# Post-norm residual of a two-layer transformer block: weights at evacuation, squares from the banks, one operation per token tile, two stores

## What is computed

```python
def _rms(x, g):
    xf = x.astype(jnp.float32)
    y = xf * lax.rsqrt(jnp.mean(xf * xf, axis=-1, keepdims=True) + EPS)
    return (y * g.astype(jnp.float32)).astype(x.dtype)

for l in range(DEPTH_2):
    mod = (silu_c @ w_ada[l] + b_ada[l])[:, None, :]
    ...
    y = _merge(o_lat[0], o_lat[1], o_lat[2], lam, lam_init, g_diff_sub[l]) @ w_out[l]
    x = x + gt_a * _rms(y, g_attn_post[l])
    ...
    hf = _rms(x, g_ffn_pre[l]) * (1.0 + sc_f) + sh_f
    x = x + gt_f * _rms(_swiglu(hf, w_ffn_gate[l], w_ffn_up[l], w_ffn_down[l]), g_ffn_post[l])
```

## Time and profile before

| | us |
|---|---|
| median of three runs (2558.07 to 2560.07) | 2558.24 |
| the profiled execution: time | 2554.62 |
| the profiled execution: span | 2552.9 |
| PE busy (share of the span) | 2240.4 (88%) |
| DVE busy | 1735.4 (68%) |
| ACT busy | 1151.7 (45%) |
| POOL busy | 53.4 (2%) |
| mean granted TensorE clock | 0.93 |

### The profile page before, as it was taken

How to read it: one execution, slowest core, us unless ns; L and a number is a source line. 1 busy time by engine, 2 the same in 40 slices (tenths; PEclk the granted TensorE clock), 3 DMA queues, 4 the chain that set the end, 5 groups by cost and what they waited for, 6 DMA issues and landing times.

```text
span 2552.9 us, 37972 instructions
## 1 busy us (share of the span) xinstructions
PE 2240.4 (88%) x14746; PEld 2009.0 (79%) x14746; DVE 1735.4 (68%) x3402; ACT 1151.7 (45%) x1907; POOL 53.4 (2%) x65
## 2 busy tenths in 40 slices
PE   3897789999999999988878789699979978797997
PEld 3887689999988888887757566599879967566996
DVE  5665558889988887767675565577666665664554
ACT  2532244555555554534344345444444444354443
POOL 1000000000000000000000000000000000000000
PEclk9998889999999999989977869799999999898999
DMA  7636545664468887767532100377657743102653
GB/s 278 196 127 205 177 147 180 220 218 135 145 197 283 268 278 235 245 188 227 181 126 77 35 33 17 124 229 235 213 183 246 256 160 115 58 1 89 186 187 117
DMA packets 137971, 435.04 MB, mean 170 GB/s; under 512 B 15360, under 2 KB 38144, under 8 KB 137280
## 3 DMA queue, kind: packets, MB, share of 16 engines
q1 hardware_dynamic: 109424, 396.93, 48.1%
q10 hardware_dynamic: 25776, 23.97, 2.8%
q0 software_dynamic: 2592, 11.70, 1.2%
HBM read 418.91 MB, written 13.63 MB: 169 GB/s over the span
## 4 chain that ended last, share of the span: by engine, by line
PE 65%; DVE 14%; issue 10%; ACT 7%; DMA 3%; POOL 1%; ACTq 0%; POOLq 0%; DVEq 0%; SPq 0%
PE bk L1650 63%; DVE SPL L1082 4%; PE bk L1656 3%; ACT SPL L737 2%; DVE R L1082 2%; ACT R L739 1%; DVE R L1091 1%; ACT R L737 1%; DVE ST L1097 1%; DVE RAW L1116 1%; POOL ST L639 1%; DMA RAW<-in_ada 1%; DVE R L1088 1%; DVE R L1086 1%; DMA RAW<-in_peer 1%
## 5 line engine op out<-in xcount | busy, mean ns | idle before, releaser
L1082 DVE TENSOR_TENSOR SPL<-RAW,SPL 128x1024 fp32r<-128x1024 f32 (+1 forms) x614 | 742.7, 1219 | 388.2 <-ACT SPL L737 387.2
L737 ACT ACTIVATE SPL<-RAW 128x1024 fp32r<-128x1024 f32 (+1 forms) x614 | 638.8, 1051 | 387.9 <-PE bk L1650 294.5
L1650 PE MATMUL bk<-HH,SPL 128*128 128x256 f32 x3840 | 753.3, 290 | 47.0 <-DVE SPL L1082 38.5
L1650 PEld LDWEIGHTS bk<-HH,SPL 128*128 128x128 f32 x3840 | 623.9, 195 | 61.0 <-issue 30.0
L1650 PE MATMUL bk<-SPL,WHL 128*128 128x512 f32 x2328 | 553.2, 392 | 13.2 <-DVE SPL L1082 9.5
L1650 PE MATMUL bk<-HL,SPL 128*128 128x256 f32 x1920 | 548.7, 286 | 0.0
L1650 PEld LDWEIGHTS bk<-SPL,WHL 128*128 128x128 f32 x2328 | 431.2, 189 | 103.7 <-issue 13.1
L1650 PE MATMUL bk<-SPL,HH 128*128 128x256 f32 (+1 forms) x1664 | 335.0, 303 | 62.9 <-DVE SPL L1082 48.3
L1650 PEld LDWEIGHTS bk<-HL,SPL 128*128 128x128 f32 x1920 | 374.3, 195 | 1.9 <-issue 0.2
L1650 PEld LDWEIGHTS bk<-SPL,HH 128*128 128x128 f32 x1664 | 285.2, 211 | 72.9 <-issue 55.9
L737 ACT ACTIVATE R<-bk 128x512 f32<-128x512 f32 (+5 forms) x376 | 186.6, 508 | 341.1 <-PE bk L1650 309.9
(11 more groups left out here) (126 smaller groups left out, 1993.6 us busy)
## 6 DMA issues: line engine op xcount, KB each, us to landing
RAW<-in_peer SPq DMA_DIRECT2D x256, 512.0 KB, 4.8
RAW<-in_ada SPq DMA_DIRECT2D x144, 512.0 KB, 4.7
RAW<-in_ffn SPq DMA_DIRECT2D x132, 512.0 KB, 4.0
RAW<-in_win SPq DMA_DIRECT2D x96, 512.0 KB, 4.4
RAW<-in_ffd SPq DMA_DIRECT2D x66, 512.0 KB, 4.2
RAW<-in_wout SPq DMA_DIRECT2D x32, 512.0 KB, 4.0
kept<-TMP ACTq DMA_DIRECT2D x88, 128.0 KB, 3.4
TMP<-kept ACTq DMA_DIRECT2D x66, 128.0 KB, 5.3
```

The lines of the kernel that those rows point to most:

```text
L737: ins = e.activation(out, in_, func, bias=bias, scale=scale)
L1082: e.tensor_tensor(out, a, b, op).then_inc(*dve.up(*points))
L1650: ins = e.matmul(out, lhsT, rhs, start=start, stop=stop, skip_group_check=True)
```

## The change

In words, beside the diff:

- `op` and `fo`: DVE multiplies the bank by gB while writing it to oY. ACT squares the unscaled bank, tile by tile, with row sums into eight small columns of ST: for `op` after DVE (two squares of 256 columns), for `fo` it starts with banks 2 and 3 while DVE has 0 and 1, then they swap. `an_a` adds the columns up (one small reduction on DVE) and has no part on ACT any more. A bank is free when both engines have read it.
- `an_b`: one operation per token tile, LX = oY*r + LX, in place of two.
- The list: `sil2` of layer 1 stands 16 steps ahead of the end of the attention of (0,0), `sil3` after the third step of `out_steps(0, 1)`; no ada chunk stands among the products and norms of (0,1) any more, and 24 of them are woven with the feed-forward part of (0,1) alone (before, 26 steps of `last`, two of them the sil steps, were woven with all three).
- The output is stored by two DMAs, one per token tile.

```diff
--- before.py
+++ after.py
@@ -236,7 +236,7 @@
     first, l0, l1 = ("ada",), ("ada2", 0), ("ada2", 1)
     fill = ada_steps(first, range(16, 48)) + [("A2",)]
     late = ada_steps(l0, range(16)) + [("mods", 0, "a")] + ada_steps(l0, range(16, 48))
-    last = [("sil2", 1), ("sil3", 1)] + ada_steps(l1, range(48))
+    last = ada_steps(l1, range(48))
     plan = [("sil",)] + ada_steps(first, range(6)) + [("norm_a", "h1")] + ada_steps(first, range(6, 12))
     plan += [("norm_b", "h1")] + ada_steps(first, range(12, 16)) + [("A1",), ("mix_in",)]
     plan += [("nT", "h1", i, k) for i in range(2) for k in range(2)] + [("alr",)]
@@ -309,11 +309,12 @@
     peer += late + [("mods", 0, "f")]
     plan += peer[:cut] + weave(peer[cut:], ctx)
     chain = [("peer_out",), ("norm_a", "fin"), ("norm_b", "fin"), ("norm_a", (0, 0, "a")), ("norm_b", (0, 0, "a"))]
-    plan += weave(chain + qkv_steps(0, 0, True), attend_steps(0, 1)) + attend_steps(0, 0)
-    side = weave(out_steps(0, 1) + pre_steps(0, 1) + ffn_steps(0, 1), last[:26])
+    rows = attend_steps(0, 0)
+    plan += weave(chain + qkv_steps(0, 0, True), attend_steps(0, 1)) + rows[:-16] + [("sil2", 1)] + rows[-16:]
+    side = out_steps(0, 1)[:3] + [("sil3", 1)] + out_steps(0, 1)[3:] + pre_steps(0, 1) + weave(ffn_steps(0, 1), last[:24])
     plan += weave(out_steps(0, 0) + pre_steps(0, 0), side) + [("mods", 1, "a")]
     kv1 = qkv_steps(1, 1, False)
-    ffn = weave(ffn_steps(0, 0)[:-3], last[26:]) + [("mods", 1, "f")]
+    ffn = weave(ffn_steps(0, 0)[:-3], last[24:]) + [("mods", 1, "f")]
     plan += ffn[:60] + weave(ffn[60:], [("norm_k", (1, 1, "a")), ("norm_b", (1, 1, "a"))] + kv1[:4])
     chain = [("fo", 0, 0), ("an_a", 0, 0, "f"), ("an_b", 0, 0, "f"), ("norm_k", (1, 0, "a")), ("norm_b", (1, 0, "a"))]
     first, others = qkv_diff_first(1, 0)
@@ -623,9 +624,11 @@
                     else:
                         sp.wait_ge(T.at("times", n - NRAW))
                 e.dma_start(raw(n), source(key)).then_inc(*T.up(f"raw{n % NRAW}", 16, [("raw", n)]))
-            sp.wait_ge(T.at("x3", 1, 0, "f"))
-            e.dma_start(out_d.rearrange("b (i p) d -> p (b i) d", p=P), LX[0]).then_inc(*T.up("d_out", 16, [("stored",)]))
-            sp.wait_ge(T.at("stored"), T.at("saved"))
+            out3 = out_d.rearrange("b (i p) d -> p (b i) d", p=P)
+            for i in range(2):
+                sp.wait_ge(T.at("x3" if i else "x3a", 1, 0, "f"))
+                e.dma_start(out3[:, i, :], LX[0][:, i, :]).then_inc(*T.up(f"d_out{i}", 16, [("stored", i)]))
+            sp.wait_ge(T.at("stored", 0), T.at("stored", 1), T.at("saved"))
 
         @block.gpsimd
         def gpsimd_program(e):
@@ -1026,14 +1029,10 @@
 
             def op(l, s, j):
                 key = ("op", l, s, j)
-                act.wait_ge(T.at("full", key))
-                A(v2(QS[(l, s)]["oY"], 2)[:, :, j * 256:(j + 1) * 256], v2(ps(*key), 2), ACT.Copy, ("out", key))
-
-            def an_a(l, s, k):
-                q = QS[(l, s)]
-                if k == "f":
-                    act.wait_ge(T.at("out", ("fy", l, s, 2)))
-                squares(v2(q["oY"], 2), stat(8, 2, s), q["junk"][:, 0:1024], ("an_s", l, s, k))
+                act.wait_ge(T.at("scaled", key))
+                for i in range(2):
+                    A(QS[(l, s)]["junk"][:, 512 * j + 256 * i:512 * j + 256 * i + 256], ps(*key)[:, i * 256:(i + 1) * 256], ACT.Square,
+                      *([("out", key), ("an_s", l, s, "a")] if i else []), accum=stat(40 + 4 * i + j, 1, s))
 
             def an_b(l, s, k):
                 for i in range(2):
@@ -1051,17 +1050,18 @@
                 hidden_hi((l, s, j))
 
             def fo(l, s):
-                for i in range(2):
-                    key = ("fy", l, s, 2 * i + 1)
-                    act.wait_ge(T.at("full", ("fy", l, s)))
-                    A(v2(QS[(l, s)]["oY"], 2)[:, i, 512:1024], ps(*key), ACT.Copy, ("out", key))
+                for c in (2, 3, 0, 1):
+                    key = ("fy", l, s, c)
+                    act.wait_ge(T.at("full", ("fy", l, s)) if c >= 2 else T.at("scaled", key))
+                    A(QS[(l, s)]["junk"][:, 512 * c:512 * c + 512], ps(*key), ACT.Square,
+                      ("squared", key), ("an_s", l, s, "f"), accum=stat(40 + 4 * (c // 2) + c % 2, 1, s))
 
@@ -1580,19 +1580,25 @@
                 dve.wait_ge(T.at("turned", *key))
                 tt(H[s][1][:, 2:4, :], v2(ps(*key), 2), H[s][0][:, 2:4, :].bitcast(F32), ALU.subtract, ("out", key))
 
+            def op(l, s, j):
+                key, c = ("op", l, s, j), slice(j * 256, (j + 1) * 256)
+                dve.wait_ge(T.at("full", key), T.at("gB", l, s, "a", 1))
+                tt(v2(QS[(l, s)]["oY"], 2)[:, :, c], v2(ps(*key), 2),
+                   QS[(l, s)]["gB"][:, c].unsqueeze(1).to_broadcast([P, 2, 256]), ALU.mult, ("scaled", key))
+
             def an_a(l, s, k):
+                parts = v2(stat(40, 8, s), 2)[:, :, 0:4 if k == "a" else 2]
                 dve.wait_ge(T.at("an_s", l, s, k))
+                rsum(stat(8, 2, s), parts, ALU.add)
+                dve.wait_ge(dve.own)
                 mean_eps(stat(8, 2, s), D, "an", l, s, k)
 
             def an_b(l, s, k):
                 q, a, r, y = QS[(l, s)], stat(8, 2, s), stat(10, 2, s), stat(12, 2, s)
                 newton(r, y, a, "an", l, s, k)
-                dve.wait_ge(T.at("gB", l, s, k, 1))
                 for i in range(2):
-                    yi = v2(q["oY"], 2)[:, i, :]
-                    stt(yi, yi, r[:, i:i + 1], q["gB"], ALU.mult, ALU.mult)
-                    dve.wait_ge(dve.own)
-                    tt(LX[s][:, i, :], LX[s][:, i, :], yi, ALU.add, ("x3" if i else "x3a", l, s, k))
+                    stt(LX[s][:, i, :], v2(q["oY"], 2)[:, i, :], r[:, i:i + 1], LX[s][:, i, :], ALU.mult, ALU.add,
+                        ("x3" if i else "x3a", l, s, k))
 
             def fs(l, s, j):
                 key = (l, s, j)
@@ -1604,17 +1610,17 @@
                 hidden_lo((l, s, j))
 
             def fo(l, s):
-                for i in range(2):
-                    key = ("fy", l, s, 2 * i)
-                    dve.wait_ge(T.at("full", ("fy", l, s)))
-                    cp(v2(QS[(l, s)]["oY"], 2)[:, i, 0:512], ps(*key), ("out", key))
+                for c in range(4):
+                    key, h = ("fy", l, s, c), slice(512 * (c % 2), 512 * (c % 2) + 512)
+                    dve.wait_ge(T.at("full", ("fy", l, s)) if c < 2 else T.at("squared", key), T.at("gB", l, s, "f", 1))
+                    tt(v2(QS[(l, s)]["oY"], 2)[:, c // 2, h], ps(*key), QS[(l, s)]["gB"][:, h], ALU.mult, ("scaled", key))
 
@@ -1642,7 +1648,8 @@
                 turn[rotation] = n + 1
                 b = rotation[n % len(rotation)]
                 if b in held:
-                    pe.wait_ge(T.at("out", held[b]))
+                    pe.wait_ge(*([T.at("squared", held[b]), T.at("scaled", held[b])] if held[b][0] == "fy" else
+                                 [T.at("out", held[b])]))
                 held[b], T.bank[key] = key, b
                 return bk[b][:, :]
 
```

4 lines of the change are left out of this document (2 added, 2 removed).

## The result

The changed kernel took 2521.84 us in the median (4 runs, 2517.65 to 2526.01), the kernel before 2558.15 beside it: a ratio of 0.9858 (95% interval 0.9838 to 0.9878), 36 us less. The prediction had 2530, from 2520 to 2542, and "faster" with 0.96.

The account below looks back on a forecast made before the run. PE's own work was taken as the bound (busy 88%), only its waits winnable; seven gains less one loss gave 28.0 us, so 2526.6 against the profiled 2554.62, plus 3.6 for the median: 2530, range 2520 to 2542.

Parts of the forecast that it names:

- Part 1: Silu and ada chunk after layer 0's attention: PE's wait near 1600 us falls from 7.5 to 1.1; gain 8.0 us.
- Part 2: Chain of (0,1) after attention: mean 1.0 us earlier, residual 2.5 us shorter, other queue changes; gain 3.9 us.
- Part 3: `an_b` of (0,0), mid feed-forward (0,1): PE's 4.74 us wait loses two residual additions; gain 2.4 us.
- Part 4: End of feed-forward (0,1): mean 0.9 us earlier, residual 2.5 shorter; gain 3.4 us of an 11.59 us wait.
- Part 5: End of feed-forward (0,0): mean 1.6 us earlier, residual 2.5 shorter; PE's 9.02 us wait shrinks by 4.1.
- Part 6: Chain of (1,0): 1.0 us from the mean and 2.5 from the residual; gain 3.5 us.
- Part 7: End of the kernel: mean 0.7 us earlier, residual 2.5, second store 0.6; gain 3.8 us.
- Part 8: Costs: longer `op` evacuation delays high splits, added ada chunks on DVE are hidden; loss 1.1 us, up to 3.3.
- A: Rival near 1600 us: the Silu wait only moves, gaining 2 to 4 us there instead of 8; 2535 us, chance 0.14.
- C: Rival: DVE's single queue bounds the feed-forward part of (0,1), making the kernel slower; 2586 us, chance 0.02.
- D: Rival: no effect, since the loads take back the saved waits; 2556 to 2560 us, chance 0.02.
- B: Rival: shorter waits keep the clock up and the second store hides; 34 us gained, 2524 us, chance 0.12.

Follow-up runs that it names:

- list alone: Kernel before with only the step list of after; evacuation, squares, residual and store as before: 2544.49 us, ratio 0.9965.
- after with one more pass: After with one more 1024-column DVE operation, into an unread buffer, ahead of each residual operation: 2540.26 us, ratio 0.9942.
- two more: After with two more 1024-column DVE operations, into an unread buffer, ahead of each residual operation: 2554.05 us, ratio 1.0005.

## Why the prediction was right, and where its sum was off

Put together, the runs give the gain in parts, each against the kernel next to it:

| part | forecast | by medians | by the trace |
|---|---|---|---|
| list (before, list alone) | 8.4 | 11, by the ratio 9 | 10.3 up to the norm (0,1), 3.9 to the end |
| residual in one operation (after with one more pass, and half of two more) | 14.9 | 16 to 18.5 | 15.9, and 33.2 for two |
| second store | 0.6 | 0.7 and 2 | 1.2, 1.2 and 1.9 |
| evacuation and squares (list alone against after with one more pass, less the store) | 4.1 | 2 to 5 | 4.1, not run alone |

The 4.1 of the last row is 6.0 from the touched code to the end less 1.9 for the store. Nearly all of it lies in two long stages, the mean at the end of feed-forward (0,0) and the mean of the chain (1,0), whose lengths move by as much between profiles of one kernel; that it equals the forecast is luck.

- **Part 1 was right.** Wait 1.1 forecast, 1.12 measured. With the 5.6 us added by which this profile reaches the touched code sooner, the last `op` of (0,1) ends at 1621.6, forecast 1621.5. The load again cost its own length: Silu began 1.30 us after the load did. The Trainium skill, "ScalarE: Activation LUTs", section "What ACT_TABLE_LOAD costs", has 1.38 more for the switch; the trace has no room for it: in after the gB copy ended 0.02 us ahead of the load and the Silu began 0.02 behind its end, and before the Silu followed as closely.
- **Part 2 was right in sum, two terms apart.** Full bank to mean 1.81 and not 1.95, and the 0.7 that I charged for the ada chunk ahead of the last bank was not paid: DVE ended that sum at 1616.07, the bank was full at 1616.05. That is most of the 1.0 us by which the first stage beat its forecast. But the 1.0 that I put down to the evacuation here was paid back within the stage, as the list alone shows; what made up for it was that the list alone gave 9.25 in this stage and not 7.3.
- **Part 3**: the wait of 4.74 became 2.58; forecast 2.3.
- **Part 4**: 11.59 became 7.80; forecast 8.2.
- **Part 5**: 9.02 became 4.60; forecast 5. The residual in it and the squares are as counted; a stage at a lower clock hides it in this pair, below. In after with one store the stage up to the mean took 118.4 us, 2.3 less than before.
- **Part 6**: the norm stage -2.5 and the mean's stage, 1.19 in its last part, as forecast (1.0).
- **Part 7**: mean 1.04 earlier where I had 0.7, residual 2.5, store 1.2 where I had 0.6. The squares were too dear: the activations of the earlier trace rows with 0.475 and 0.69 are no squares but the exponentials of the attention, which read a bias from `ST`; the new squares took 0.38 and 0.60. On the store the page that I cited beside it, the Trainium skill, "DMA: Bandwidth & Descriptors", section "Anatomy of one DMA — SWDGE (gpsimd) path", gave an estimate of 1.4. Its figure is for transfers that GpSimd issues, and SyncE issues this one. Measured 1.2 in the direct pairs, so the estimate was nearer than the end of the bounds that I chose; 512 and 256 KB both landing in 2.7 us fits a fixed part as well, but one landing of 512 KB in 3.6 shows how loose this is.
- **Part 8 failed on one wait.** `op` (0,0,1) cost 1.49 us where I had 1.1, `op` (0,0,2) and (0,0,3) nothing. But "7 us more over 215 us are hidden: nothing" was wrong. The mean load of DVE did not decide, the order of steps near the end of the part did. The same piece of PE before:

```profile
1866.78 2.98 PE L1650 MATMUL bk<-SPL,WHL 128*128 128x512 f32 x12 [1.22 <-DVE SPL L1082]
```

Its wait of 1.22 became 2.26, and its 12 matmuls took 4.58 us instead of 2.98, in a window with the clock at 0.73 where before had 1.00. These 2.6 us are most of why feed-forward (0,1) came out 1 us longer and not 2.2 shorter. The list alone has the same wait; ending the chunks early takes it away. The sum of an ada chunk is not what PE waited for, though. Before the change it stood directly ahead of that low part on DVE, and there was no wait for WHL; after, it comes behind. DVE before, then ACT and DVE after:

```profile
1863.89 1.22 DVE L1116 CUSTOM_DVE_ANT_0 RAW<-RAW,TMP 128x1024 f32<-128x1024 f32 x1
...
1865.03 0.42 DVE L1082 TENSOR_TENSOR WHL<-R,WHL 128x256 fp32r<-128x256 f32 x1
```

```profile
1845.93 1.06 ACT L740 ACTIVATE SPL<-RAW 128x1024 fp32r<-128x1024 f32 x1
1846.87 1.50 ACT L740 ACTIVATE R<-bk,MOD,AB 128x128 f32<-128x128 f32 x4
...
1848.71 0.43 DVE L1082 TENSOR_TENSOR WHL<-R,WHL 128x256 fp32r<-128x256 f32 x1 [0.23 <-ACT WHL L740]
1849.05 1.22 DVE L1116 CUSTOM_DVE_ANT_0 RAW<-RAW,TMP 128x1024 f32<-128x1024 f32 x1
```

The low part waited for ACT, where a high split of 1.06 us now stands ahead of the four `nT` activations and of the high part of the hidden values (before, no split stood there). In after with the chunks ended early the same split stands there, but PE has 24 of the 48 first products of the block still to do behind the first transposes, and no wait. So the moved chunks changed the order of the other steps around them; which neighbour counts was not run apart.

The forecast of the difference, 28 us, is about what the touched part shows. From there to the end before took 1008.4 us, after 983.5 and 982.3, and after with one store 976.8, which its second store would make 975.6: 25, 26 and 33 us less, 28 in the mean. That the mean meets the forecast is partly luck, with a spread of 8 us. This spread comes more from the clock than from waits. At the end of feed-forward (0,0), after has the same three waits as before (1.03, 2.62 and 1.90 us), and yet PE did fewer matmuls in the same busy time. The granted clock is the third number from the right. Before and after, the 20 us in which that begins:

```profile
2050.00:2070.00 20.00, 16.35 (x122) 15.19 (x121) 11.36 (x17) 9.68 (x17) 0.00 (x0) 1.00 0.53 174
```

```profile
2030.00:2050.00 20.00, 16.35 (x110) 15.13 (x109) 11.14 (x15) 8.68 (x15) 0.00 (x0) 0.91 0.54 174
```

The absolute number was 8 us too high for a second reason. I had put the forecast for the median 3.6 above the sum because three runs of before stood that much above the profiled execution. In 12, 21 and 15 later runs its medians were 2555.7, 2554.5 and 2554.2, so the profiled 2554.62 was the typical one and the 3.6 should not have been added. The sum against it, 2526.6, is 5 from the result.

Of the rivals, A (the Silu wait moves) is out by the 1.12. C (DVE becomes the bound) is out: the kernel is faster, and at its one new wait DVE was itself waiting for ACT. D (no effect) is out by the time. B forecast 34 us by a clock that stays up and a hidden second store, and 34 is what was measured. Its reasons are half there: after the wait near 1600 the clock did stay at 1.00, and the store gave more. But nothing shows that shorter waits in general keep the clock up: the extra passes cost little more than their waits, and at the end of feed-forward (0,0) it was before that had the higher clock. The remaining 6 or so of the 34 us, 3 of them ahead of the touched code, stay open between chance and the program as a whole.

## What to carry to other kernels

In a chain that all engines wait for, each operation is paid in full: two large DVE operations fewer gave 2.5 us at each of six places, 15 to 16 us together, while moving chunks of other work from one place to another changed nothing in sum. Multiply by a gain where the data leaves the bank anyway, and sum the squares there too; but see first what stands ahead of that evacuation in each engine's queue, since a bank that now needs two engines can close a circle with a step that waits for the first.

When work is woven into a part whose engine has room on average, look at the last two blocks of the part by themselves, in the queue of every engine: the woven steps shift the other steps as well. And size a forecast for the median by many runs of the kernel before, or by the profiled execution itself, not by three runs.

## What the runs showed of the hardware

- A square read from a bank with immediate operands took 0.38 us for 256 columns and 0.60 for 512, against 0.475 and 0.688 for exponentials that read a bias from `ST`. The Trainium skill, "ScalarE: Activation LUTs", section "What ACT_TABLE_LOAD costs", puts 0.093 us on each such operand, and its formula gives 0.40 and 0.61; the trace agrees, and the forecast would have been closer by it.
- The same code took 113.4 to 119.3 us in one attention stage. Within it PE was busy for the whole of the 10 us from 1520, in one profile with 67 matmuls at a granted clock of 0.92 and in another with 36 at 0.50. The runs of one kernel spread by up to 9 us. A gain of 3 us does not show in the median of a few runs; stages of a trace can show it, where their granted clocks are the same.
- Stores of 512 KB landed in 2.6 to 2.7 us and once in 3.6; 1024 KB in 4.7 to 4.9 in three profiles and in 4.0 in a fourth; 256 KB in 2.7 behind others.
